# Layer 2's up projections: the passes of the high and the low half of h with the weight's high half made one pass of 512 columns, on one Trainium2 core

## The chip, the cores and the metric

The kernel runs on one core of one Trainium2 chip. The metric is device time in microseconds (us), the median of three runs. Nothing else runs on the chip.

## What is computed

A trunk of two layers over 256 tokens with 2048 features, all in float32. Layer 1 mixes tokens with attention, layer 2 with causal pooling; each layer then has a gated channel mixer, and that of layer 2 is what the change touches:

```python
def conv_ffn(h, w_up, conv_w, conv_b, w_down):     # h 256 x 2048, w_up 2048 x 11264, w_down 5632 x 2048
    u = h @ w_up
    up = jnp.pad(u, ((0, 0), (CONV_WIDTH - 1, 0), (0, 0)))
    y = conv_b
    for i in range(CONV_WIDTH):                    # CONV_WIDTH = 3
        y = y + up[:, i:i + S] * conv_w[i]
    a, g = jnp.split(y, 2, axis=-1)
    return (jax.nn.silu(g) * a) @ w_down
...
mod = cond @ w_mod[l] + b_mod[l]                   # adaLN: shift, scale, gate from c
sh1, sc1, g1, sh2, sc2, g2 = jnp.split(mod, N_MOD, axis=-1)
x = x + g2[:, None, :] * conv_ffn(h, w_up[l], conv_w[l], conv_b[l], w_down[l])
```

## The kernel before

**Split products.** TensorE multiplies in the type fp32r. Each operand is therefore split into a high half (rounded to fp32r) and a low half (the remainder), and a product is made of three passes: high by high, low by high, high by low. The activations are `h_hi` and `h_lo`, the weights `w_hi` and `w_lo`. The helper `sub` holds the three passes of the up projections (L633, L634, L635), each with 256 columns; `unit_tok` holds those of the down projections (L661 to L663), each with 512 columns.

**Units.** Weights arrive in units of 512 rows by 512 columns (1 MB, one DMA of SP into one of the four slots of `raw`). A unit is worked through in two halves. For each half ScalarE writes `w_hi` and VectorE then writes `w_lo` (both in their function `split`), into one of four half-unit slots; the half-unit four places on may be split only when TensorE is done with the old one, which `sub_used` counts. So at the moment when TensorE ends a unit u, the splits stand at the last half of unit u+2, and in the program of ScalarE and VectorE `split(.., j + 2)` stands at the step of unit j.

**Groups, pairs and blocks.** Four units make a group: 512 channels by 256 tokens, in two PSUM banks (`bank_tile`: two tiles of 256 to a bank), slot 0 in banks 0 and 1, slot 1 in banks 2 and 3. A pair (`up_pair`) is a group of a and a group of g, eight units. Layer 2 has three blocks: four pairs and then the down projection of their channels, four pairs and theirs, three pairs and theirs. That makes 11 pairs and 88 up units. The first block is written out pair by pair; the other two run as loops (`Fori`).

**After a group.** ScalarE makes the convolution's last tap with the bias out of PSUM (`conv_last_tap`), VectorE adds the other two taps out of PSUM (`conv_taps`, L1640) and thereby frees the banks (`bank0_free`, `bank1_free`). After a group of g follow the silu (ScalarE), the product with a (VectorE, L1690), `g_hi` (ScalarE) and `g_lo` (VectorE, L1694); only behind them, in the program of both engines, stands the split of the next pair's third unit. Every activation of ScalarE carries the line L1023 of its helper.

**The modulation gate.** In the first block of layer 2 VectorE also works on the last four chunks of `w_mod`, one with each pair: `piece` adds up products (L1376) at the steps 1, 2, 5 and 6 of the pair, L1380 adds the two halves, TensorE sums over the partitions (`gate_sum`, L707, one fp32 matmul that takes its place behind the pair), and VectorE adds the bias (`gate_row`, L1394), behind the `g_lo` of the pair. `gate_sum` writes bank 4, 5 or 6, which the up projections don't use.

The waits that matter here, of TensorE ahead of a group and of `gate_sum`, and VectorE's `gate_row`:

```python
def group_slot_free(g):
    pe.wait_ge(bank0_free, g - 1)
    pe.wait_ge(bank1_free, g - 1)
def gate_sum(c_all, a):
    pe.wait_ge(mod_added, c_all + 1)
    pe.wait_ge(mod_ready, c_all)
...
    dve.wait_ge(mod_red, c_all + 1)
    dve.wait_ge(gate_bias, 16 if c_all < 24 else 32)
    V.tensor_tensor(grow_mlp[...], ps[:, (4, 5, 6, 4)[cg], :],
                    grow_mlp[...], ALU.add).then_inc(mod_ready, 1)
```

Of the kernel before, what the change touches and what calls it, by code (L numbers as in the profile page):

```python
# [22 lines left out]
ALU = mybir.AluOpType  # L23
# [5 lines left out]
P = 128  # L29
# [5 lines left out]
def decoder_trunk(nc, x, c, w_mod, b_mod, norm_gain, w_attn_in, b_forget, w_attn_out, w_pool,  # L35
# [36 lines left out]
    with ExitStack() as ctx:  # L72
# [7 lines left out]
        h_hi = sb("h_hi", [P, KT, SEQ], F32R)  # L80
        h_lo = sb("h_lo", [P, KT, SEQ], F32R)
# [56 lines left out]
        tmpn = work[:, 2048:3072].rearrange("p (t n) -> p t n", t=4)  # L138
        junk = work[:, 2048:3072].rearrange("p (a n) -> p a n", a=QT)
# [35 lines left out]
        def pool_bank(gr, a):  # L175
# [8 lines left out]
                   3: ((2, 3), (4, 5), (6, 7), (2, 3))}  # L184

        GATE_BANKS = {0: (4, 5, 6, 4), 1: (4, 5, 6, 7), 2: (4, 5, 6, 7)}
# [61 lines left out]
        conv_tap = sem("conv_tap")  # L248
        silu_done = sem("silu_done")
# [368 lines left out]
        def _(pe):  # L618
# [46 lines left out]

            def unit_raw(pos):
# [36 lines left out]
            def gate_sum(c_all, a):  # L703

                pe.wait_ge(mod_added, c_all + 1)
                pe.wait_ge(mod_ready, c_all)
                mm(ps[:, (4, 5, 6, 4)[c_all % 4], :], ones[:, :], macc[:, a, 0, :],  # L707
                   start=True, stop=True).then_inc(mod_red, 1)
# [11 lines left out]
            def transposes(n, c):  # L720
# [5 lines left out]
                elif n == 2:  # L726
# [189 lines left out]
            def mlp(l):  # L916
# [4 lines left out]
                def chunk_sum(quad, j):  # L921
                    c = MLP_SUM.get(mlp_step(quad, j)) if l == 0 else None
                    if c is not None and c < 24:
                        gate_sum(c, (c + 1) % 2)
                    elif c is not None:
                        mod_sum(c, (c + 1) % 2, NH)

                for g0, n in BLOCKS:
                    last_block = n == 3

                    def up_pair(i):
                        first = isinstance(i, int) and i == g0 == 0
                        for half in range(2):
                            group_slot_free(g + 2 * i + half)
                            if first and half:
                                pe.wait_ge(t_ready, KT * nm + KT)
                            for ks in range(4):
                                if l == 0:
                                    chunk_sum(q + 2 * i + half, ks)
                                unit(q + 2 * i + half, ks, 4 * ks, ks == 0, ks == 3, h_hi, h_lo, half,  # L940
                                     h_need=KT * nm)
# [12 lines left out]
                    g += 2 * n  # L954
                    if not last_block:
                        for i in range(2):
                            for half in range(2):
                                group_slot_free(g + 2 * i + half)
                                for ks in range(4):
                                    chunk_sum(q + 2 * i + half, ks)  # L960
                                    pe.wait_ge(glo_ready, 2 * (gi + g0 + ks + 1))
                                    unit_tok(q + 2 * i + half, ks, 4 * ks, ks == 0, ks == 3, g_hi, g_lo, half)
                        q += 4
                        g += 4
                    else:
                        for cg in range(4):
                            group_slot_free(g + cg)
                            for ks in range(3):
# [3 lines left out]
                                unit_tok(q + u // 4, u % 4, 4 * ks, ks == 0, ks == 2, g_hi, g_lo, cg % 2)  # L972
# [43 lines left out]
            pe.wait_ge(gate_ready, 8)  # L1016
            gate_rows(2, lambda k: prm[:, FGAIN + k:FGAIN + k + 1])
# [3 lines left out]
        def _(act):  # L1021
# [235 lines left out]
            def conv_last_tap(l, used, dst, first_tile, slot, need):  # L1257
# [3 lines left out]
                for t in range(4):  # L1261
                    A(dst[:, t, :], bank_tile(slot, t), ACT.Identity,
# [3 lines left out]
            def mlp(l):  # L1266
# [8 lines left out]
                for g0, n in BLOCKS:  # L1275

                    def up_pair(i):
                        for half in range(2):
                            for ks in range(4):
# [8 lines left out]
                                if not (first and j < 2):  # L1288
                                    split(q + 2 * i, j + 2)
                                if ks == 3:  # L1290
                                    conv_last_tap(l, 8 * q + 16 * i + 8 * (half + 1), (ya, yg)[half],
                                                  4 * i + (4 * g0 + FT * half), half,
                                                  2 * i + (2 * (gi + g0) + 1))

                        for b in range(2):
                            act.wait_ge((bank0_free, bank1_free)[b], g + 2 * i + 2)
# [46 lines left out]
        def _(dve):  # L1343
# [45 lines left out]
            def gate_row(c_all):  # L1389
# [4 lines left out]
                V.tensor_tensor(grow_mlp[:, 512 * cg:512 * cg + 512], ps[:, (4, 5, 6, 4)[cg], :],  # L1394
# [236 lines left out]

            def conv_taps(l, dst, first_tile, slot, c0):

                for b in range(2):
                    dve.wait_ge(conv_act, c0 + 2 * b + 2)
                    for tap, sh in ((1, 1), (0, 2)):
                        for t in (2 * b, 2 * b + 1):
                            if tap == 0:
                                dve.wait_ge(conv_tap, c0 + t + 1)
                            i = V.scalar_tensor_tensor(  # L1640
                                dst[:, t, sh:SEQ], bank_tile(slot, t)[:, 0:SEQ - sh],
# [4 lines left out]
                    i.then_inc((bank0_free, bank1_free)[b], 1)  # L1646

            def mlp(l):
# [15 lines left out]
                for g0, n in BLOCKS:  # L1664
                    last_block = n == 3

                    def up_pair(i):
                        for half in range(2):
                            for ks in range(4):
# [12 lines left out]
                                if l == 0:  # L1682
                                    chunk_bias(q + 2 * i, j)
                                if ks == 3:
                                    conv_taps(l, (ya, yg)[half], 4 * i + (4 * g0 + FT * half), half,
                                              8 * i + (8 * (gi + g0) + 4 * half))
                        for b in range(2):
                            dve.wait_ge(silu_done, 2 * i + (2 * (gi + g0) + b + 1))
                            dve.wait_ge((bank0_free, bank1_free)[b], g + 2 * i + 1)
# [7 lines left out]
                        if l == 1 and g0 == 0:  # L1697
                            gate_row(i + ch)

# [124 lines left out]
```

## Time and profile before

| | us |
|---|---|
| median of three runs | 2100.67 (2097.5 to 2101.4) |
| the profiled execution | 2103.21 |
| its span, first to last instruction | 2101.6 |
| TensorE busy | 2033.4 (97%) |
| VectorE busy | 1631.1 (78%) |
| ScalarE busy | 1011.7 (48%) |
| mean granted clock of TensorE | 0.992 |

The profile lists each engine's busy time, the groups of instructions by line, and the waits. In a timeline each row gives the start of an instruction (or of several merged ones) in us from the start of the span, its length, the engine, the line and the operation, how many there are, and in brackets the engine's idle time just ahead and what ended it. Matmuls overlap in such rows: the distance between two starts is what one costs, not the length of one.

### The profile page before, as it was taken

What the parts mean: (1) busy time and instruction counts of PE and PEld (TensorE: products, weight loads), DVE (VectorE), ACT (ScalarE), POOL (GpSimd) and SP (SyncE); (2) the same over time, 40 slices, a digit from 0 to 9 for tenths busy, and PEclk for the clock granted to TensorE, in tenths of its full rate; (3) what the DMA queues carried; (4) which work ended last, traced back from release to release, by engine and by line L of the source; (5) the groups of instructions that cost most, each with busy time, mean ns of one, the idle gap of its engine ahead of it and who ended that gap; (6) DMA issues with size and microseconds to landing.
All of it is one profiled execution on the core that took longest, in us unless ns stands there. A gap on an engine that the chain in (4) does not pass through costs nothing.

```text
span 2101.6 us, 36721 instructions
## 1 busy us (share of the span) xinstructions
PE 2033.4 (97%) x13730; PEld 1879.5 (89%) x13730; DVE 1631.1 (78%) x2277; ACT 1011.7 (48%) x1347; POOL 308.0 (15%) x459
## 2 busy tenths in 40 slices
PE   3999999999999999999999999899999999999998
PEld 3888989888999889999899987799988999889986
DVE  5776888887899988898989977888865566555565
ACT  4323674554554444554445555554443454434453
POOL 3232432220111222112212100011000000000000
PEclk9999999999999999999999999999999999999999
DMA  9999899885788999888998874387655555565552
GB/s 360 356 350 330 297 325 322 284 307 203 271 315 315 331 344 340 306 304 314 357 340 309 314 280 149 122 301 280 241 195 186 182 184 185 189 198 164 199 180 100
DMA packets 235842, 558.28 MB, mean 266 GB/s; under 512 B 14024, under 2 KB 15032, under 8 KB 235192
## 3 DMA queue, kind: packets, MB, share of 16 engines
q1 hardware_dynamic: 180408, 355.03, 48.7%
q0 software_dynamic: 55296, 201.35, 26.9%
q8 instruction: 94, 1.54, 0.3%
q14 instruction: 44, 0.36, 0.0%
HBM read 554.23 MB, written 2.10 MB: 265 GB/s over the span
## 4 chain that ended last, share of the span: by engine, by line
PE 83%; DVE 7%; issue 3%; ACT 3%; DMA 3%; SPq 1%; DVEq 0%; ACTq 0%; POOLq 0%
PE ps L633 16%; PE ps L635 15%; PE ps L634 15%; PE ps L661 10%; PE ps L663 10%; PE ps L662 10%; DVE w_lo L1362 2%; PE ps L681 2%; DVE macc L1376 1%; DMA mraw<-in_w_mod 1%; PE ps L699 1%; PE ps L678 1%; ACT w_hi L1023 1%; DMA work<-in_conv_b 1%; DVE work L1640 1%
## 5 line engine op out<-in xcount | busy, mean ns | idle before, releaser
L1023 ACT ACTIVATE w_hi<-raw 128x1024 fp32r<-128x1024 f32 x640 | 666.4, 1056 | 778.9 <-PE ps L635 485.7
L1362 DVE TENSOR_TENSOR w_lo<-raw,w_hi 128x1024 fp32r<-128x1024 f32 x640 | 766.3, 1223 | 346.4 <-ACT w_hi L1023 345.7
L633 PE MATMUL ps<-h_hi,w_hi 128*128 128x256 f32 x3200 | 914.7, 286 | 3.5 <-DVE w_lo L1362 2.9
L635 PE MATMUL ps<-h_hi,w_lo 128*128 128x256 f32 x3200 | 908.1, 284 | 0.0
L634 PE MATMUL ps<-h_lo,w_hi 128*128 128x256 f32 x3200 | 908.1, 284 | 0.0
L633 PEld LDWEIGHTS ps<-h_hi,w_hi 128*128 128x128 f32 x3200 | 616.8, 193 | 7.5 <-issue 6.9
L634 PEld LDWEIGHTS ps<-h_lo,w_hi 128*128 128x128 f32 x3200 | 617.0, 193 | 1.9 <-issue 1.7
L635 PEld LDWEIGHTS ps<-h_hi,w_lo 128*128 128x128 f32 x3200 | 616.7, 193 | 0.0
L1376 DVE SCALAR_TENSOR_TENSOR macc<-mraw,cond,macc 128x512 f32<-128x512 f32 x620 | 427.3, 745 | 50.5 <-DMA mraw<-in_w_mod 43.9
L518 POOL DMA_DIRECT2D mraw<-in_w_mod x358 | 258.7, 723 | 1184.4 <-DVE macc L1376 869.7
L661 PE MATMUL ps<-w_hi,g_hi 128*128 128x512 f32 x832 | 326.1, 392 | 1.5 <-DVE w_lo L1362 1.5
L663 PE MATMUL ps<-w_hi,g_lo 128*128 128x512 f32 x832 | 324.0, 389 | 0.0
L662 PE MATMUL ps<-w_lo,g_hi 128*128 128x512 f32 x832 | 323.8, 389 | 0.0
L661 PEld LDWEIGHTS ps<-w_hi,g_hi 128*128 128x128 f32 x832 | 156.2, 188 | 34.3 <-issue 2.6
L663 PEld LDWEIGHTS ps<-w_hi,g_lo 128*128 128x128 f32 x832 | 156.2, 188 | 32.9
L662 PEld LDWEIGHTS ps<-w_lo,g_hi 128*128 128x128 f32 x832 | 156.3, 188 | 32.0 <-issue 0.2
L1640 DVE SCALAR_TENSOR_TENSOR work<-ps,prm,work 128x255 f32<-128x255 f32 (+1 forms) x352 | 141.0, 472 | 0.0
L1023 ACT ACTIVATE macc<-mraw,cond 128x512 f32<-128x512 f32 x96 | 63.8, 713 | 60.2 <-DMA mraw<-in_w_mod 60.2
L1023 ACT ACTIVATE work<-ps,prm 128x256 f32<-128x256 f32 x176 | 84.3, 558 | 0.0
L1023 ACT ACTIVATE work<-work 128x512 f32<-128x512 f32 (+1 forms) x68 | 40.4, 595 | 68.6 <-DVE work L1640 47.1
L681 PE MATMUL ps<-work,raw 128*128 128x256 f32 x256 | 57.7, 387 | 3.3 <-DMA raw<-in_w_attn_in 3.3
L681 PEld LDWEIGHTS ps<-work,raw 128*128 128x128 f32 x256 | 49.7, 195 | 10.5 <-issue 3.3
(164 smaller groups left out, 1141.3 us busy)
## 6 DMA issues: line engine op xcount, KB each, us to landing
mraw<-in_w_mod POOLq DMA_DIRECT2D x358, 512.0 KB, 6.6
raw<-in_w_up SPq DMA_DIRECT2D x176, 1024.0 KB, 5.7
raw<-in_w_down SPq DMA_DIRECT2D x88, 1024.0 KB, 5.6
raw<-in_w_attn_in SPq DMA_DIRECT2D x48, 1024.0 KB, 9.0
raw<-in_w_attn_out SPq DMA_DIRECT2D x16, 1024.0 KB, 7.0
work<-in_w_mod POOLq DMA_DIRECT2D x12, 512.0 KB, 8.7
early<-in_w_mod POOLq DMA_DIRECT2D x8, 512.0 KB, 12.6
raw<-in_w_pool SPq DMA_DIRECT2D x4, 1024.0 KB, 5.4
```

What stands on the lines that cost most here:

```text
L518: pool.dma_start(slot, w_mod[l, 256 * j:256 * j + 256, ds(512 * c_l, 512)] .rearrange("(k p) n -> p k n", p=P)).then_inc(landed, 16)
L633: mm(o, wh, ah, start=st, stop=False, skip_group_check=True)
L634: mm(o, wh, al, start=False, stop=False, skip_group_check=True)
L635: i = mm(o, wl, ah, start=False, stop=last_half and kk == 1, skip_group_check=True)
L661: mm(o, ah, w_hi[:, s, kk, :], start=st, stop=False)
L662: mm(o, ah, w_lo[:, s, kk, :], start=False, stop=False)
L663: i = mm(o, al, w_hi[:, s, kk, :], start=False, stop=sp_)
L681: i = mm(bank_tile(slot, t), w[:, t * P:(t + 1) * P], xnT[:, k, :], start=st and t % 2 == 0, stop=sp_, skip_group_check=True)
L1023: return nc.scalar.activation(o, i, f, **kw)
L1362: V.tensor_tensor(w_lo[:, s, :, :], raw[:, j % 4, h * 1024:(h + 1) * 1024].rearrange("p (k n) -> p k n", k=2), w_hi[:, s, :, :].bitcast(F3 ...
L1376: V.scalar_tensor_tensor(macc[:, a, kk, :], mod_slot(c_all, j)[:, kk, :], cond[:, k:k + 1], macc[:, a, kk, :], ALU.mult, ALU.add).then_inc ...
L1640: i = V.scalar_tensor_tensor(dst[:, t, sh:SEQ], bank_tile(slot, t)[:, 0:SEQ - sh], prm[:, ds(first_tile + CWcol(l, tap) + t, 1)], dst[:, t ...
```

## The change

In layer 2's up projections the passes L633 and L634 become one. `h_hi` and `h_lo` are now the two halves of one array `h_both`, and one matmul of 512 columns (256 of the high half, 256 of the low) multiplies both with `w_hi`. Its output fills a whole PSUM bank: columns 0 to 255 hold high by high, 256 to 511 low by high. The pass with `w_lo` still has 256 columns and adds into columns 0 to 255. A group so takes four banks instead of two: slot 0 is banks 0 to 3, slot 1 banks 4 to 7.

On the way out ScalarE copies the upper 256 columns into `wide` in SBUF (`wide_copy`, two instructions of 512 elements), VectorE adds the lower ones out of PSUM (`wide_add`, two instructions) and frees the banks, and both the last tap and the other taps read `wide`. `wide` is there once, so the copy waits until the taps of the group before are done (`taps0_done`, `taps1_done`).

As all eight banks are in use, `gate_sum` moves to bank 3: TensorE issues it ahead of the second half of the pair's last unit, VectorE's `gate_row` moves to step 7, between `split` and `wide_add`, and TensorE waits ahead of the next pair, and ahead of the first down projection, until `gate_row` has read the bank. Other banks move along: the transposes at the start of layer 2's channel mixer, the down projections of layer 2 (four slots in turn) and the final gain's rows.

```diff
-        h_hi = sb("h_hi", [P, KT, SEQ], F32R)
-        h_lo = sb("h_lo", [P, KT, SEQ], F32R)
+        h_both = sb("h_both", [P, 2, KT, SEQ], F32R)
+        h_hi, h_lo = h_both[:, 0], h_both[:, 1]
...
-                   3: ((2, 3), (4, 5), (6, 7), (2, 3))}
-        GATE_BANKS = {0: (4, 5, 6, 4), 1: (4, 5, 6, 7), 2: (4, 5, 6, 7)}
+                   3: ((4, 5), (6, 7), (4, 5), (6, 7))}
+        GATE_BANKS = {0: (4, 5, 6, 4), 1: (4, 5, 6, 7), 2: (0, 1, 2, 3)}
...
+            def unit_wide(q, j, k0, first, last, slot, h_need, gate_chunk=None):
+                for h in range(2):
+                    pe.wait_ge(hlo_ready, h_need + k0 + 2 * h + 2)
+                    if h and gate_chunk is not None:
+                        gate_sum(gate_chunk, 0, 3)
+                    low, s0 = split_at(q, j)
+                    pe.wait_ge(lo_ready, low + h + 1)
+                    s = (s0 + h) % 4
+                    for kk in range(2):
+                        k = k0 + 2 * h + kk
+                        for t in range(4):
+                            wh, wl = (w[:, s, kk, t * P:(t + 1) * P] for w in (w_hi, w_lo))
+                            o = ps[:, 4 * slot + t, :]
+                            mm(o.rearrange("p (c n) -> p c n", c=2), wh, h_both[:, :, k, :],
+                               start=first and h == 0 and kk == 0, stop=False, skip_group_check=True)
+                            i = mm(o[:, 0:SEQ], wl, h_hi[:, k, :], start=False, stop=last and h == 1 and kk == 1,
+                                   skip_group_check=True)
+                    i.then_inc(sub_used, 1)
...
+                            if l == 1 and g0 == 0 and not first and half == 0:
+                                pe.wait_ge(mod_ready, i + ch)
...
-                        if l == 1 and g0 == 0:
-                            gate_sum(i + ch, 0)
...
+                    if l == 1 and g0 == 0:
+                        pe.wait_ge(mod_ready, 48)
...
-                                    unit_tok(q + 2 * i + half, ks, 4 * ks, ks == 0, ks == 3, g_hi, g_lo, half)
+                                    unit_tok(q + 2 * i + half, ks, 4 * ks, ks == 0, ks == 3, g_hi, g_lo, half + 2 * l * i)
...
             pe.wait_ge(gate_ready, 8)
+            group_slot_free(G_FFN[1] + 33)
...
+            def wide_copy(used, slot, n):
+                act.wait_ge(sub_used, used)
+                for b in range(2):
+                    if not (isinstance(n, int) and n == 0):
+                        act.wait_ge((taps0_done, taps1_done)[b], n)
+                    A(wide[:, 2 * b:2 * b + 2, :], ps[:, 4 * slot + 2 * b:4 * slot + 2 * b + 2, SEQ:2 * SEQ],
+                      ACT.Copy).then_inc(wide_copied, 1)
...
                 for t in range(4):
-                    A(dst[:, t, :], bank_tile(slot, t), ACT.Identity,
+                    if l and t % 2 == 0:
+                        act.wait_ge((bank0_free, bank1_free)[t // 2], freed)
+                    A(dst[:, t, :], wide[:, t, :] if l else bank_tile(slot, t), ACT.Identity,
...
+            def wide_add(slot, n):
+                for b in range(2):
+                    dve.wait_ge(wide_copied, 2 * n + b + 1)
+                    V.tensor_tensor(wide[:, 2 * b:2 * b + 2, :], ps[:, 4 * slot + 2 * b:4 * slot + 2 * b + 2, 0:SEQ],
+                                    wide[:, 2 * b:2 * b + 2, :], ALU.add).then_inc((bank0_free, bank1_free)[b], 1)
...
                                     split(q + 2 * i, j + 2)
...
+                                if l == 1 and g0 == 0 and j == 7:
+                                    gate_row(i + ch)
+                                if ks == 3 and l == 1:
+                                    wide_add(half, 2 * i + (2 * g0 + half))
                                 if ks == 3:
                                     conv_taps(l, (ya, yg)[half], 4 * i + (4 * g0 + FT * half), half,
...
-                        if l == 1 and g0 == 0:
-                            gate_row(i + ch)
```

## Rows read from the trace of the kernel before

**Rows 1.** Waits of PE, 1450 to 2102 us: in total, times, longest (us).

```profile
PE ps L661 <- DVE w_lo L1362: 0.7, 1, 0.7
```

**Rows 2.** Timeline, PE, an up unit: first passes of two neighbouring units.

```profile
1650.07 0.28 PE L633 MATMUL ps<-h_hi,w_hi 128*128 128x256 f32 x1
...
1655.82 0.28 PE L633 MATMUL ps<-h_hi,w_hi 128*128 128x256 f32 x1
```

**Rows 3.** Timeline, PE, a down projection: two passes, 24 apart.

```profile
1593.63 0.39 PE L661 MATMUL ps<-w_hi,g_hi 128*128 128x512 f32 x1
...
1599.07 0.39 PE L661 MATMUL ps<-w_hi,g_hi 128*128 128x512 f32 x1
```

**Rows 4.** Timeline, PE, first pair of layer 2: starts of its fourth and fifth unit.

```profile
1355.29 0.36 PE L633 MATMUL ps<-h_hi,w_hi 128*128 128x256 f32 x1 [0.71 <-DVE w_lo L1362]
...
1361.53 0.35 PE L633 MATMUL ps<-h_hi,w_hi 128*128 128x256 f32 x1 [0.26 <-DVE w_lo L1362]
```

**Rows 5.** Timeline, DVE: the split that the first wait of rows 4 ended with.

```profile
1353.92 2.36 DVE L1362 TENSOR_TENSOR w_lo<-raw,w_hi 128x1024 fp32r<-128x1024 f32 x2 [0.46 <-ACT w_hi L1023]
```

**Rows 6.** Timeline, PE, end of the first block's second pair.

```profile
1431.44 0.28 PE L635 MATMUL ps<-h_hi,w_lo 128*128 128x256 f32 x1
1431.56 1.02 PE L707 MATMUL ps<-macc,ones 128*128 128x512 f32 x2
```

**Rows 7.** Timeline, ACT, the same end.

```profile
1431.76 1.06 ACT L1023 ACTIVATE w_hi<-raw 128x1024 fp32r<-128x1024 f32 x1 [1.82 <-PE ps L635]
```

**Rows 8.** Timeline, DVE, the same pair: the two halves of macc added.

```profile
1425.24 0.69 DVE L1380 TENSOR_TENSOR macc<-macc 128x512 f32<-128x512 f32 x1
```

**Rows 9.** Timeline, ACT, end of a pair in a loop (second block).

```profile
1705.70 1.06 ACT L1023 ACTIVATE w_hi<-raw 128x1024 fp32r<-128x1024 f32 x1 [1.82 <-PE ps L635]
1706.67 1.91 ACT L1023 ACTIVATE work<-ps,prm 128x256 f32<-128x256 f32 x4
...
1711.27 0.63 ACT L1023 ACTIVATE work<-work 128x512 f32<-128x512 f32 x1 [0.93 <-DVE work L1640]
...
1713.30 2.94 ACT L1023 ACTIVATE w_hi<-raw 128x1024 fp32r<-128x1024 f32 x3
```

**Rows 10.** Timeline, DVE, the same end.

```profile
1706.88 1.23 DVE L1362 TENSOR_TENSOR w_lo<-raw,w_hi 128x1024 fp32r<-128x1024 f32 x1 [1.65 <-ACT w_hi L1023]
1708.03 3.21 DVE L1640 SCALAR_TENSOR_TENSOR work<-ps,prm,work 128x255 f32<-128x255 f32 x8
...
1714.47 3.49 DVE L1362 TENSOR_TENSOR w_lo<-raw,w_hi 128x1024 fp32r<-128x1024 f32 x3 [0.20 <-ACT w_hi L1023]
```

**Rows 11.** Groups of instructions by form, ACT, whole span: count | busy us, mean ns.

```profile
L1023 ACT ACTIVATE work<-ps,prm 128x256 f32<-128x256 f32 x176 | 84.3, 558 | 0.0
...
L1023 ACT ACTIVATE h_hi<-work 128x256 fp32r<-128x256 f32 x64 | 25.5, 418 | 35.3 <-DVE work L1441 34.9
L1023 ACT ACTIVATE work<-ps 128x512 f32<-128x512 f32 x30 | 16.7, 592 | 17.5 <-PE ps L663 6.5 <-PE ps L716 6.4 <-PE ps L825 2.8
...
L1023 ACT ACTIVATE g_hi<-ps 128x256 fp32r<-128x256 f32 x16 | 5.8, 367 | 0.0
```

**Rows 12.** The same view, 1450 to 2102 us, DVE: gate_row.

```profile
L1394 DVE TENSOR_TENSOR work<-ps,work 128x512 f32<-128x512 f32 x2 | 1.4, 684 | 0.0
```

**Rows 13.** Timeline, PE: the only wait of the last two blocks.

```profile
2034.73 0.47 PE L661 MATMUL ps<-w_hi,g_hi 128*128 128x512 f32 x1 [0.70 <-DVE w_lo L1362]
```

**Rows 14.** Timeline, PE: two gaps elsewhere in the kernel.

```profile
79.30 1.02 PE L699 MATMUL ps<-ones,macc 128*128 128x1 f32 x8 [2.23 <-DVE mods L1386]
...
1286.80 2.05 PE L737 MATMUL ps<-ident,work 128*128 128x128 f32 x16 [1.91 <-DVE work L1423]
```

**Rows 15.** Windows behind those gaps: length, PE busy (instructions), PEclk, DMA share, GB/s.

```profile
80.00:84.00 4.00, 4.00 (x26) 0.69 1.04 389
84.00:88.00 4.00, 4.00 (x18) 0.89 1.04 387
...
1288.00:1292.00 4.00, 2.82 (x17) 1.00 0.00 0
```

More of the change, by code:

```diff
@@ L138, in decoder_trunk @@
         tmpn = work[:, 2048:3072].rearrange("p (t n) -> p t n", t=4)
+        wide = work[:, 2048:3072].rearrange("p (t n) -> p t n", t=4)
         junk = work[:, 2048:3072].rearrange("p (a n) -> p a n", a=QT)
@@ L725, in transposes @@
                     pe.wait_ge(gate_ready, 2 * n + 2 * c + 2)
-                elif n == 2:
+                elif n == 2 or n == 3 and c >= 2:
                     pe.wait_ge(t_ready, n * KT + 4 * c - 4)
@@ L923, in chunk_sum @@
                     if c is not None and c < 24:
-                        gate_sum(c, (c + 1) % 2)
+                        gate_sum(c, (c + 1) % 2, (4, 5, 6, 4)[c % 4])
                     elif c is not None:
@@ L939, in up_pair @@
                                     chunk_sum(q + 2 * i + half, ks)
-                                unit(q + 2 * i + half, ks, 4 * ks, ks == 0, ks == 3, h_hi, h_lo, half,
-                                     h_need=KT * nm)
+                                    unit(q + 2 * i + half, ks, 4 * ks, ks == 0, ks == 3, h_hi, h_lo, half,
+                                         h_need=KT * nm)
+                                else:
+                                    unit_wide(q + 2 * i + half, ks, 4 * ks, ks == 0, ks == 3, half, KT * nm,
+                                              i + ch if g0 == 0 and half == 1 and ks == 3 else None)
                                 if first and half == 0 and ks < 2:
                                     transposes(nm, ks + 2)
-                        if l == 1 and g0 == 0:
-                            gate_sum(i + ch, 0)
                     if l == 0 or g0 == 0:
@@ L971, in mlp @@
                                 pe.wait_ge(glo_ready, 2 * (gi + g0 + ks + 1))
-                                unit_tok(q + u // 4, u % 4, 4 * ks, ks == 0, ks == 2, g_hi, g_lo, cg % 2)
+                                unit_tok(q + u // 4, u % 4, 4 * ks, ks == 0, ks == 2, g_hi, g_lo, cg if l else cg % 2)
             mlp(0)
@@ L1292, in up_pair @@
                                                   4 * i + (4 * g0 + FT * half), half,
-                                                  2 * i + (2 * (gi + g0) + 1))
+                                                  2 * i + (2 * (gi + g0) + 1), g + 2 * i + half + 1)
                         for b in range(2):
-                            act.wait_ge((bank0_free, bank1_free)[b], g + 2 * i + 2)
+                            if l == 0:
+                                act.wait_ge((bank0_free, bank1_free)[b], g + 2 * i + 2)
+                            else:
+                                act.wait_ge((taps0_done, taps1_done)[b], 2 * i + (2 * g0 + 2))
                             A(yg[:, 2 * b:2 * b + 2, :], yg[:, 2 * b:2 * b + 2, :], ACT.Silu).then_inc(silu_done, 1)
@@ L1640, in conv_taps @@
                             i = V.scalar_tensor_tensor(
-                                dst[:, t, sh:SEQ], bank_tile(slot, t)[:, 0:SEQ - sh],
+                                dst[:, t, sh:SEQ], (wide[:, t, :] if l else bank_tile(slot, t))[:, 0:SEQ - sh],
                                 prm[:, ds(first_tile + CWcol(l, tap) + t, 1)], dst[:, t, sh:SEQ],
@@ L1734, in mlp @@
                                 cg = u // 3
-                                residual(g + cg, 8 * q + 2 * u + 2, cg % 2, grow_mlp, 512 * cg, gates, before + 2 * cg)
+                                residual(g + cg, 8 * q + 2 * u + 2, cg if l else cg % 2, grow_mlp, 512 * cg, gates, before + 2 * cg)
             def boundary(n, second, third):
```

24 lines of the change are left out of this document (16 added, 8 removed).

## Prediction

> **What bounds the kernel now.** I read the page first: TensorE is busy 97% of the span. An average says little of one stage, so the waits of TensorE came next, from the middle of the changed stage to the end. There is one, of 0.7 us [rows 1]: layer 2's up and down projections run at TensorE's own pace, with VectorE and ScalarE beside them. The third view is the timeline, where the distance between starts shows that pace. A unit of up projections has 48 passes of 256 columns and takes 5.75 us [rows 2], 120 ns a pass. In the down projection 24 passes of 512 columns take 5.44 us [rows 3], 226.7 ns a pass. The granted clock is 1.00 there, which is 2.4 GHz, so the columns take 106.7 and 213.3 ns, and both sizes leave the same 13.3 ns a pass. The last views are the timelines of ScalarE and VectorE where a pair ends: they show how much room the work beside TensorE has. The change takes from TensorE and gives to those two, and adds waits of TensorE on VectorE, so this room decides.
>
> **What the change takes away.** Three passes of 256 columns (360 ns) become one of 512 and one of 256 (226.7 + 120 = 346.7 ns): 13.3 ns saved, 16 times a unit, 0.213 us a unit. For 88 units that is 18.8 us. The first four units of layer 2 gain nothing: their neighbours wait for VectorE already [rows 4], whose pace there is set by the modulation of h and by the pieces of `w_mod`, and a faster pass only lengthens those waits. That leaves 84 x 0.213 = 17.9 us. The trace has no matmul whose moving operand lies in two stretches of 256; I take its fixed part as that of the other 512-column passes, 13.3 ns, the nearest row. The bounds: nothing fixed at all for it (another 18 us saved, which no row supports, since both sizes show the 13.3), or the cost of two passes of 256, 240 ns (nothing saved).
>
> The rows leave 13.3 ns a pass. The Trainium skill, page "TensorE: Matmul & The Clock Gate", section "Back-to-back issue gap", gives columns by 2.4 GHz plus about 2.5 ns for the isolated case. By that figure the estimate of the saving would be 1344 x 2.5 ns = 3.4 us. The rows disagree, at both sizes, and the sum goes by the rows.
>
> **The new wait in the first block, four times.** `gate_row` now stands on VectorE behind both halves of `split(9)`, and the second half can only be split when TensorE has ended the pair's last unit. TensorE must not begin the next pair before `gate_row` is done. Take S as the start of that `w_hi`. TensorE would start its next pass at S - 0.20 [rows 6, 7]. VectorE starts `w_lo` at S + 1.18 and could start the next instruction at S + 2.33 [rows 9, 10]; `gate_row` takes 0.68 us [rows 12] and ends at S + 3.01. From the end of a `w_lo` that TensorE waits for (1353.92 + 1.23 = 1355.15) to the pass are 0.14 us [rows 4, 5], and the first pass costs 0.08 us more than another (0.36 for 0.28). So TensorE loses 3.01 + 0.14 + 0.08 + 0.20 = 3.4 us. Nothing covers it: behind the waiting instruction stand all passes of the next pair, and everything else waits for those. It comes three times between pairs and once ahead of the down projection: 13.7 us. The bounds of one are 3.1 (no 0.14 and no dearer pass) and 3.7 (two more semaphore waits between release and pass, at 0.14 each).
>
> `gate_sum` itself moves from behind the pair to 2.77 us ahead of its end, at the same price. It needs L1380, which ends at 1425.9, 5.6 us ahead of the pair's end [rows 6, 8]. The later taps (next part) push this by some 1.9 us and the faster passes take 0.8 us of the pair; about 1 us is left. Nothing.
>
> **The clock behind those waits.** What a gap of this length does is seen elsewhere. At 77.07 (79.30 - 2.23) TensorE stopped for 2.23 us, then had some 0.9 us of one-column matmuls, 3.1 us without dense work [rows 14]; behind it the granted clock was 0.69 and 0.89 over two stretches of 4 us [rows 15]: 4 x 0.31 + 4 x 0.11 = 1.7 us lost. After 1.91 us and transposes it stayed at 1.00 [rows 14, 15]. The new gaps are 3.3 us with dense passes on both sides, longer than the one that was followed by a lower clock. I take 1.65 us for each of four: 6.6 us. Bounds: 0 and 8.
>
> **The longer chain behind every group.** Before, from S: `w_lo` starts at 1.18, the taps at 2.33, they end at 5.54, the second silu starts at 5.57, ScalarE comes to the `w_hi` of the next pair's third unit at 7.60, and its `w_lo` ends at 1714.47 + 1.23 = S + 10.00 [rows 9, 10]. TensorE wants it at S - 0.20 + 2 x 5.75 = S + 11.3: 1.3 us of room. With the change: ScalarE's copies (592 ns [rows 11]) run beside `w_lo`. VectorE's adds, whose nearest row is `gate_row` with 684 ns [rows 12], start at 2.33 and 2.93 and end at 3.01 and 3.61. ScalarE's last tap starts at 3.10, and VectorE's taps need two of its four tiles. One takes 558 ns from PSUM at a distance of 0.45 [rows 9, 11]; from SBUF I add 0.05, the difference of 418 and 367 for the same 256 elements [rows 11]. So two are done at 3.10 + 0.50 + 0.61 = 4.2, VectorE starts at 4.3 and ends at 7.5, 1.95 us later than before. The path from there on (silu, product, `g_hi`, `w_hi`, `w_lo`) is unchanged, so this `w_lo` ends at S + 11.95. TensorE, now faster, wants it at S - 0.20 + 2 x 5.547 = S + 10.9. With 0.14 and 0.08 on top it loses 1.27 us. In the second and third block that happens behind five pairs: 6.4 us. Behind the second block's last pair the two units are down units of 5.44 us, and the loss is 1.5. Behind the third block's last pair the kernel waits already [rows 13], so the whole 1.95 comes on top. Sum 9.8 us. Bounds, with the lengthening between 1.7 and 2.1: 8 and 11. The four pairs of the first block don't pay, since TensorE is 3.4 us late there. Behind a group of a nothing waits: the same shift meets over 4 us of room there, as no silu and no product stand in between.
>
> **Edits at nothing.** The banks of the transposes, of the down groups and of the final rows: their waits are for work that ended units ago. VectorE and ScalarE get 44 instructions each, some 30 and 26 us beside a TensorE of over 600 us; what of that lies on the path is in the chain above. Transfers need no more than before.
>
> **Sum.** -17.9 + 13.7 + 6.6 + 9.8 = +12.2 us. On the profiled execution (2103.21, its span 2101.6 and 1.6 around it) that gives 2115.4; it ran 2.5 us above the median of the runs, so on the median, 2100.67 + 12.2 = 2112.9 us, 0.6% slower.
>
> **Rivals.** (a) The clock stays up behind the four waits: +5.6 us, 2106.3. For it: 1.91 us left it up, and no row shows a pure gap between 2.3 and 3.2 us. Against it: the row at 79.30. In between lie cases where it falls once to three times; they belong to the forecast's range. (b) The other side: the evictions are hidden. If adds and taps overlap so well that the chain gets longer by less than the 0.7 us at which `w_lo` is still in time (S + 10.7 against S + 10.9), the 9.8 us are gone but for a part of the last pair's, and -17.9 + 13.7 + 6.6 + 0.7 = +3.1 us remain, 2103.8; with the clock up as well, -3.5 us, 2097.2. Against it: the last tap's wait for the add, in series on two engines. (c) The wide pass costs what two cost, because its operand lies in two stretches: nothing saved, +30 us, 2131. For it only that no row shows such an operand. The same mechanism in part is the case in which a pass has a fixed cost of 2.5 ns instead of 13.3, the rest going with the columns: 3.4 saved, 2127. The page "TensorE: Matmul & The Clock Gate" of the Trainium skill, quoted above, has that figure.
>
> **How the numbers follow.** Forecast with one to four falls of the clock, 0.62; clock up, 0.15; evictions hidden, 0.12, half of it with the clock up; wide pass dear, 0.04 (0.02 of it by the figure of 2.5 ns); 0.07 for gains I don't see. The range for 8 in 10: the low end leaves out the hidden evictions with the clock up, and takes the clock-up case with the low bounds, -17.9 + 12.4 + 8 = +2.5, 2103; the high end is all high bounds, -17.9 + 14.8 + 8 + 11 = +15.9, rounded up to 2118 for a saving a little under 13.3 ns. 0.2% is 4.2 us, about what a measurement here can tell from no change. Slower by more: the forecast, two thirds of the clock-up case and the dear pass, 0.76. Within: the rest of clock-up, most of the hidden evictions, 0.14. Faster: 0.10.
>
> **What the profile will show.** Distances of 226.7 and 120 ns in the up units and 5.55 us from unit to unit. Four waits of about 3.2 us of TensorE on L1394's successor (`gate_row`), three ahead of an up pass, one ahead of a down pass, each with a stretch at the lower clock level (1.2 GHz) behind. Seven waits on `w_lo`, about 1.1 us each, ahead of the third unit behind a pair of the second and third block. The second silu starting 7.5 us behind S. What would make it wrong: the order of `gate_row` and `split` on VectorE read wrongly, ScalarE's last tap not held up by the add, or a different distance of the wide passes.

## The result and the profile after

| kernel | median us | ratio to before (95% interval) |
|---|---|---|
| before | 2100.88 | |
| changed | 2116.63 | 1.0082 (1.007 to 1.0094) |

The changed kernel is 15.8 us slower; 2112.9 was forecast. The times here and below leave out one of the seven executions of the kernel with the early split, which had a mean granted clock of 0.455 and took 4474 us. The profiled execution of the changed kernel took 2115.76 us, with a span of 2114.1. The page of that execution, busy time by engine and its share of the span:

```profile
PE 2027.9 (96%) x12322; PEld 1806.0 (85%) x12322; DVE 1659.0 (78%) x2321; ACT 1037.3 (49%) x1391; POOL 308.9 (15%) x459
```

TensorE has 1408 passes less to do and is busy 5.5 us less, yet the span is longer. So the time went into waits, and part of what is still counted as busy into a lower clock. The waits of TensorE from 1300 us on (total, times, longest):

```profile
PE ps L684 <- DVE w_lo L1407: 15.8, 10, 3.2
...
PE ps L665 <- DVE w_lo L1407: 4.1, 2, 2.8
PE ps L665 <- DVE work L1439: 3.0, 1, 3.0
```

Before there was 0.7 us of these in the last 650 us [rows 1], and 1.0 in the first pair [rows 4]. L684 is the wide pass, L665 the first pass of the down projection, L1439 is `gate_row`. A wait is put down to what came last by the records: in three of them it says `w_lo`, although the wait in the program is that on `gate_row`. The timelines of TensorE, ScalarE and VectorE at the end of the first pair show it:

```profile
1379.85 0.28 PE L686 MATMUL ps<-h_both,w_lo 128*128 128x256 f32 x1
1383.29 0.47 PE L684 MATMUL ps<-h_both,w_hi 128*128 128x512 f32 x1 [3.16 <-DVE w_lo L1407]
```

```profile
1380.17 1.06 ACT L1052 ACTIVATE w_hi<-raw 128x1024 fp32r<-128x1024 f32 x1 [2.52 <-PE ps L686]
```

```profile
1381.26 1.22 DVE L1407 TENSOR_TENSOR w_lo<-raw,w_hi 128x1024 fp32r<-128x1024 f32 x1 [2.35 <-ACT w_hi L1052]
1382.40 0.68 DVE L1439 TENSOR_TENSOR work<-ps,work 128x512 f32<-128x512 f32 x1
```

`gate_row` ends at 1383.08, TensorE starts at 1383.29. Without the wait it would have started at 1379.97, 0.12 us behind the start of the last narrow pass. Windows of TensorE over the same place (length, busy and count, granted clock, DMA share, GB/s):

```profile
1380.00:1384.00 4.00, 0.84 (x5) 0.96 0.84 295
1384.00:1388.00 4.00, 4.00 (x16) 0.61 0.73 261
1388.00:1392.00 4.00, 4.00 (x25) 1.00 0.00 0
```

Behind the wait the clock fell to its lower level (1.2 GHz) for part of two stretches: 4 x 0.04 + 4 x 0.39 = 1.7 us. The same came behind the second of these waits and, for longer, around the end of the third, not behind the fourth.

The end of a pair in a loop, with ScalarE first and VectorE below it (they answer to [rows 9, 10]):

```profile
1668.19 1.06 ACT L1052 ACTIVATE w_hi<-raw 128x1024 fp32r<-128x1024 f32 x1 [1.76 <-PE ps L686]
1669.15 1.07 ACT L1052 ACTIVATE work<-ps 128x512 f32<-128x512 f32 x2
1671.38 2.08 ACT L1052 ACTIVATE work<-work,prm 128x256 f32<-128x256 f32 x4 [1.16 <-DVE work L1681]
...
1675.90 0.63 ACT L1052 ACTIVATE work<-work 128x512 f32<-128x512 f32 x1 [0.94 <-DVE work L1692]
...
1677.94 3.90 ACT L1052 ACTIVATE w_hi<-raw 128x1024 fp32r<-128x1024 f32 x4
```

```profile
1669.37 1.23 DVE L1407 TENSOR_TENSOR w_lo<-raw,w_hi 128x1024 fp32r<-128x1024 f32 x1 [1.59 <-ACT w_hi L1052]
1670.51 1.28 DVE L1681 TENSOR_TENSOR work<-ps,work 128x512 f32<-128x512 f32 x2
1672.62 3.25 DVE L1692 SCALAR_TENSOR_TENSOR work<-work,prm 128x255 f32<-128x255 f32 x8 [0.83 <-ACT work L1052]
...
1679.11 4.63 DVE L1407 TENSOR_TENSOR w_lo<-raw,w_hi 128x1024 fp32r<-128x1024 f32 x4 [0.20 <-ACT w_hi L1052]
```

Here S is 1668.19. ScalarE stands idle for 1.16 us until VectorE has added (L1681), VectorE for 0.83 us until ScalarE has made the last tap. The taps start at S + 4.43 (before 2.33), the second silu at S + 7.71 (5.57), and the third unit's `w_lo` ends at S + 12.15 (10.00). TensorE waits:

```profile
1679.19 0.28 PE L686 MATMUL ps<-h_both,w_lo 128*128 128x256 f32 x1
1680.39 0.50 PE L684 MATMUL ps<-h_both,w_hi 128*128 128x512 f32 x1 [0.93 <-DVE w_lo L1407]
```

Last, the pace. A couple of a wide and a narrow pass, read as the distance of wide passes over 32 couples, ahead of the wait at 1680.39 and behind the one at 1726.81:

```profile
1667.64 0.40 PE L684 MATMUL ps<-h_both,w_hi 128*128 128x512 f32 x1
...
1678.95 0.40 PE L684 MATMUL ps<-h_both,w_hi 128*128 128x512 f32 x1
...
1728.65 0.40 PE L684 MATMUL ps<-h_both,w_hi 128*128 128x512 f32 x1
...
1739.74 0.40 PE L684 MATMUL ps<-h_both,w_hi 128*128 128x512 f32 x1
```

The first two rows give 353.4 ns a couple, the other two 346.6. Three passes of 256 columns took 360 ns. The waits cut the stage into eleven stretches of about a pair each. Read in the same way, three of them (the second and third pair, and 1726.81 to 1772.59) ran at 346.7 and the other eight at 353.3. A stretch kept its distance from one wait to the next, but for the eight couples that stand between a `gate_sum` and the end of its pair: they ran at 346.7 in all four pairs of the first block.

### The profile page after: what moved, and what is told of

Its sections match the earlier page's. It is cut to its first block, busy times and chain, and to the rows that moved or that the text cites. A ratio compares the mean times of both kernels' runs of the same rounds, so it can differ in the third digit from the quotient of the medians.

```text
span 2114.1 us, 34059 instructions
## 1 busy us (share of the span) xinstructions
PE 2027.9 (96%) x12322; PEld 1806.0 (85%) x12322; DVE 1659.0 (78%) x2321; ACT 1037.3 (49%) x1391; POOL 308.9 (15%) x459
## 4 chain that ended last, share of the span: by engine, by line
PE 83%; DVE 7%; ACT 4%; issue 4%; DMA 2%; DVEq 0%; POOL 0%; ACTq 0%; POOLq 0%
PE ps L684 13%; PE ps L665 10%; PE ps L667 9%; PE ps L666 9%; PE ps L637 9%; PE ps L638 9%; PE ps L639 9%; PE ps L686 7%; PE ps L705 3%; DVE w_lo L1407 2%; ACT w_hi L1052 2%; PE ps L702 1%; PE ps L723 1%; DVE macc L1421 1%; ACT work L1052 1%
## 5 line engine op out<-in xcount | busy, mean ns | idle before, releaser
L684 PE MATMUL ps<-h_both,w_hi 128*128 128x512 f32 x1408 | 503.6, 402 | 16.5 <-DVE w_lo L1407 15.8
L637 PE MATMUL ps<-h_both,w_hi 128*128 128x256 f32 x1792 | 513.4, 287 | 1.5 <-DVE w_lo L1407 1.3
L638 PE MATMUL ps<-h_both,w_hi 128*128 128x256 f32 x1792 | 508.5, 284 | 0.0
L639 PE MATMUL ps<-h_both,w_lo 128*128 128x256 f32 x1792 | 508.3, 284 | 0.0
L686 PE MATMUL ps<-h_both,w_lo 128*128 128x256 f32 x1408 | 396.8, 282 | 0.0
L637 PEld LDWEIGHTS ps<-h_both,w_hi 128*128 128x128 f32 x1792 | 345.2, 193 | 3.6 <-issue 3.1
L638 PEld LDWEIGHTS ps<-h_both,w_hi 128*128 128x128 f32 x1792 | 345.4, 193 | 1.3 <-issue 1.2
L639 PEld LDWEIGHTS ps<-h_both,w_lo 128*128 128x128 f32 x1792 | 345.4, 193 | 0.0
L684 PEld LDWEIGHTS ps<-h_both,w_hi 128*128 128x128 f32 x1408 | 267.2, 190 | 85.4 <-issue 13.7
L665 PE MATMUL ps<-w_hi,g_hi 128*128 128x512 f32 x832 | 325.9, 392 | 7.7 <-DVE w_lo L1407 4.7
L686 PEld LDWEIGHTS ps<-h_both,w_lo 128*128 128x128 f32 x1408 | 268.4, 191 | 1.0 <-issue 1.0
L665 PEld LDWEIGHTS ps<-w_hi,g_hi 128*128 128x128 f32 x832 | 156.2, 188 | 40.9 <-issue 5.9
L1692 DVE SCALAR_TENSOR_TENSOR work<-work,prm 128x254 f32<-128x254 f32 (+1 forms) x176 | 71.4, 478 | 17.9 <-ACT work L1052 17.9
```

The source lines that it names most:

```text
L637: mm(o, wh, ah, start=st, stop=False, skip_group_check=True)
L638: mm(o, wh, al, start=False, stop=False, skip_group_check=True)
L639: i = mm(o, wl, ah, start=False, stop=last_half and kk == 1, skip_group_check=True)
L665: mm(o, ah, w_hi[:, s, kk, :], start=st, stop=False)
L684: mm(o.rearrange("p (c n) -> p c n", c=2), wh, h_both[:, :, k, :], start=first and h == 0 and kk == 0, stop=False, skip_group_check=True)
L686: i = mm(o[:, 0:SEQ], wl, h_hi[:, k, :], start=False, stop=last and h == 1 and kk == 1, skip_group_check=True)
```

## The experiments

The reasons to be told apart: the four waits on `gate_row` with the clock behind them, the longer chain behind a group, and why most couples take 353.3 ns instead of 346.7. All experiments start from the changed kernel, and those that stand behind the run with both moves from that one. The kernel before, run on the same chip, had 2099.7 us (18 runs), 2099.1 (11) and 2099.7 (15) in the three sessions.

### Do two stretches make the wide pass dearer?

```diff
-        h_both = sb("h_both", [P, 2, KT, SEQ], F32R)
-        h_hi, h_lo = h_both[:, 0], h_both[:, 1]
+        h_both = sb("h_both", [P, KT, 2, SEQ], F32R)
+        h_hi, h_lo = h_both[:, :, 0], h_both[:, :, 1]
...
-                            mm(o.rearrange(...), wh, h_both[:, :, k, :],
+                            mm(o.rearrange(...), wh, h_both[:, k, :, :],
```

> The changed kernel with one difference: h_both is laid out so that the two halves of one k tile lie side by side, and the wide pass reads one stretch of 512. Theory A, two stretches make the wide pass dearer: a wide pass and its narrow one then start 346.7 ns apart in all eleven pairs (now 353.3 in most, 346.7 in some), and about 1000 such couples save 6.7 ns each, 7 us: 2110 us. Theory B, the layout has nothing to do with it (the distance comes from how passes of two lengths alternate): both distances are still there, 2113 to 2119 us. The four waits on gate_row and the seven on w_lo stay the same under both.

2119.0 us, ratio 1.0093 (1.0078 to 1.0108): theory B. Wide passes 32 couples apart, in two stretches of the second block:

```profile
1703.84 0.40 PE L684 MATMUL ps<-h_both,w_hi 128*128 128x512 f32 x1
...
1715.15 0.40 PE L684 MATMUL ps<-h_both,w_hi 128*128 128x512 f32 x1
...
1784.83 0.40 PE L684 MATMUL ps<-h_both,w_hi 128*128 128x512 f32 x1
...
1795.92 0.40 PE L684 MATMUL ps<-h_both,w_hi 128*128 128x512 f32 x1
```

The first two are 353.4 ns apart per couple, the last two 346.6, with the operand in one piece. The layout is not the cause of the long distance. The short distance now stood in other stretches: the third pair, the end of the second block and the end of the third.

### gate_row earlier

```diff
-                                if not (first and j < 2):
+                                if l == 1 and g0 == 0 and j == 7:
+                                    split(q + 2 * i, j + 2, (0,))
+                                    gate_row(i + ch)
+                                    split(q + 2 * i, j + 2, (1,))
+                                elif not (first and j < 2):
                                     split(q + 2 * i, j + 2)
...
-                                if l == 1 and g0 == 0 and j == 7:
-                                    gate_row(i + ch)
```

> The changed kernel with one difference: on VectorE, step 7 of a pair, gate_row stands between the two halves of split(9) instead of behind both. My theory: the four waits of 3.0 to 3.2 us on gate_row vanish (13.5 us), with them the falls of the clock behind them (three, 5 us), and the first block's pairs now show the wait on the third unit's w_lo that the long one covered (about 1.1 us each, 4 us in all): -14.5 us, 2102 us. Rival, the waits are held by something else (the sum of the macc halves, w_lo of the next unit): they only change their releaser, 2114 to 2117 us.

2102.7 us, ratio 1.0019 (1.001 to 1.0028). The waits of TensorE from 1300 us on:

```profile
PE ps L684 <- DVE w_lo L1407: 8.7, 10, 1.0
PE ps L665 <- DVE w_lo L1407: 5.4, 3, 2.9
```

No wait on `gate_row` is left, none of the long ones ahead of L684, and the clock stays at 1.00 through the first block. In their place the first block's pairs wait for the third unit's `w_lo` (0.78, 0.97, 0.95 and 1.18 us), as expected. 13.9 us of the 15.8 (13 by the ratios) hang on where one instruction of 0.68 us stands.

### The next split earlier

```diff
+                        if l == 1:
+                            split(q + 2 * i, 10, (0,))
                         for b in range(2):
...
-                                    split(q + 2 * i, j + 2)
+                                    split(q + 2 * i, j + 2, (1,) if l == 1 and j == 0 else (0, 1))
```

The same on ScalarE and VectorE, and in the down steps.

> The changed kernel with one difference: on ScalarE and VectorE the first half of the split of the unit three places after a pair's end stands ahead of the silu, the product, g_hi and g_lo of that pair, behind the taps. My theory (the longer chain behind a group delays that split): the seven waits on w_lo of 0.9 to 2.8 us in the second and third block vanish, -9 us, 2107.5 us; at most 0.7 us come back in the last block, where g_lo is needed soonest. Rival, VectorE and ScalarE are simply full there, and the order doesn't matter: waits of the same sum with g_lo or a later w_lo as releaser, 2115 to 2118 us.

2107.9 us, ratio 1.0034 (1.0021 to 1.0047). Waits of TensorE from 1300 us on:

```profile
PE ps L684 <- DVE w_lo L1411: 10.9, 5, 3.2
...
PE ps L665 <- DVE work L1443: 3.0, 1, 3.0
PE ps L665 <- DVE g_lo L1759: 0.9, 1, 0.9
```

The seven waits of the second and third block are gone but for 0.9 us on `g_lo`. The engines were not full; the order made the wait.

### The clock: keep TensorE at work while it waits

```diff
+            def filler():
+                for _ in range(4):
+                    mm(ps[:, 0, 0:384], ones[:, :], keep[:, :], start=True, stop=True)
...
+                                filler()
                                 pe.wait_ge(mod_ready, i + ch)
...
+                        group_slot_free(g)
+                        filler()
                         pe.wait_ge(mod_ready, 48)
```

> The changed kernel with one difference: TensorE fills each of the four waits on gate_row with four fp32 matmuls of 384 columns (2.56 us at 2.4 GHz) into bank 0, which nobody reads; the output is the same. Theory: the falls of the granted clock behind the waits come from the idle time, so the clock stays at 1.00 there, the waits shrink to about 0.6 us, the next pass starts at the same time as before: three falls of 1.7 us are saved, -5 us, 2111.5 us. Rival, the clock falls for another reason, or the falls cost nothing on the path: 2115 to 2118 us.

2112.2 us, ratio 1.0064 (1.0051 to 1.0077), 4.5 us below the changed kernel (3.8 by the ratios, whose intervals overlap). The time agrees with the theory but doesn't settle it; the trace does. The end of the first pair on TensorE, and its windows:

```profile
1378.67 2.74 PE L672 MATMUL ps<-keep,ones 128*128 128x384 f32 x8
1381.84 0.50 PE L688 MATMUL ps<-h_both,w_hi 128*128 128x512 f32 x1 [0.43 <-DVE work L1446]
```

```profile
1380.00:1384.00 4.00, 3.57 (x17) 1.00 0.72 225
1384.00:1388.00 4.00, 4.00 (x25) 1.00 0.46 176
```

With work that nobody needs, the clock stays at its upper level (2.4 GHz) behind all four waits. So the falls come from the idle engine. The Trainium skill, page "TensorE: Matmul & The Clock Gate", section "Part 1: The HAM clock gate (the "warmup" mystery)", describes just that: the lower rate is the resting state and activity lifts it. This run agrees. From the first of the four waits to the second TensorE took 49.3 us here and 50.2 in the changed kernel, although 120 of the 128 couples in between ran at 353.3 ns here and at 346.7 there. With that 0.8 us the fall cost 1.7 us, as read from the windows.

Behind another wait the clock did fall in this run. The last wait on `w_lo`, 2.84 us ahead of the third block's down projection, ends at 2040.79:

```profile
2040.00:2044.00 4.00, 3.21 (x10) 0.77 0.22 44
2044.00:2048.00 4.00, 4.00 (x16) 0.81 1.03 395
```

That is 1.7 us again. It happened in the runs with the contiguous layout, with `gate_row` earlier and with the passes in groups too (waits of 2.84, 2.86 and 2.84 us), and not in the changed kernel's profile (2.80 us).

### The passes in groups

```diff
-                        for t in range(4):
-                            ... wide pass of tile t, then narrow pass of tile t
+                        for t in range(4):
+                            ... wide pass of tile t
+                        for t in range(4):
+                            ... narrow pass of tile t
```

> The changed kernel with one difference: for each k tile the four wide passes (one for each tile of 128 output channels) come first and the four narrow ones after them, instead of wide and narrow in turn. Theory C, the 6.7 ns that most couples of a wide and a narrow pass take too long arise where a pass of the one length follows one of the other, and only in some phases of TensorE's start: with a quarter of these changes left, 4 wide and 4 narrow passes take 1387 to 1393 ns instead of 1413, 4 to 5 us less in all: 2112 us. Rival D, each wide pass of this operand is dearer by itself in that phase: the same 1413 ns, 2117 us. The eleven waits stay under both.

2116.3 us, ratio 1.0082 (1.0068 to 1.0095). By the time neither theory is refuted: the runs lie between 2112.0 and 2121.3. In the trace a group of four couples takes 1403 ns from 1655 to 1673 us and from 1925 to 1940 us, which is neither 1387 to 1393 nor 1413. There are two distances again: three of the eleven stretches ran at 1400 ns, the others at 1403. So the order changes the cost, which D alone doesn't say. But C's sum fails as well: a quarter of the changes of length is left, and 13.3 or 16.7 of the 26.7 ns, so the cost doesn't go by the number of changes. Over all couples that is only some 1 us less than in the changed kernel, too little for the times to show.

### Both moves, and both with the groups

> The changed kernel with both moves at once: gate_row between the two halves of split(9), and the first half of the next split ahead of the silu. If the waits on gate_row, the falls of the clock and the waits on w_lo are the whole loss, none of them is left but some 0.9 us for g_lo in the last block, and the kernel keeps what the passes save (6.7 to 13.3 ns for each of 1344): from the 2102.7 us with only the first move, less 7 waits of 1.2 us and 4 of about 1.1 and plus 0.9, 2091 us, ahead of the kernel before (2099.7). Rival: with the order changed the waits show up at other places of the pair, 2098 to 2104 us.

2089.0 us, ratio 0.9948 (0.9935 to 0.9961), ahead of the kernel before by 10 us. All waits of TensorE from 1300 us on in this kernel (L761 is there in every version):

```profile
PE ps L761 <- ACT work L1052: 5.1, 1, 5.1
PE ps L684 <- DVE w_lo L1411: 1.4, 2, 1.0
PE ps L665 <- DVE g_lo L1761: 0.9, 1, 0.9
PE ps L1024 <- DVE work L1490: 0.8, 1, 0.8
```

The waits and the clock behind them were the whole loss. With the passes in groups on top:

> Both moves of the run before and the passes in groups (four wide, four narrow). Theory C: 4 to 8 us below the run with the two moves alone, since the whole 13.3 ns for each couple are saved less a rest: 2085 us. Rival D: the same as that run, 2091 us.

2085.5 us, ratio 0.9939 (0.9926 to 0.9952): the best version, 0.6% under the kernel before. The 3.5 us to the run before it lie within the two intervals, and the groups are worth less than that. Counted from the first transposes of layer 2's channel mixer to the end of the span, which leaves out the part where the two programs are the same, they take 759.3 us and 758.5 us (spans 2089.2 and 2082.5):

```profile
1329.91 3.65 PE L761 MATMUL ps<-ident,work 128*128 128x128 f32 x16 [5.07 <-ACT work L1052]
```

```profile
1324.08 3.48 PE L762 MATMUL ps<-ident,work 128*128 128x128 f32 x16 [5.07 <-ACT work L1053]
```

In the kernel with both moves alone, some 390 of the 1344 couples behind the first four units have 346.7 ns and the others 353.3; in groups all have 350.8, which makes 0.8 us.

### The wide pass undone, the rest kept

```diff
-                            mm(o.rearrange(...), wh, h_both[:, :, k, :], start=..., stop=False, ...)
+                            mm(o[:, 0:SEQ], wh, h_hi[:, k, :], start=..., stop=False, ...)
+                            mm(o[:, SEQ:2 * SEQ], wh, h_lo[:, k, :], start=False, stop=False, ...)
```

> The kernel with both moves (gate_row and split early), and the wide pass undone alone: two passes of 256 columns take its place, each with its own half of h and its own half of the bank, the rest (banks, copies, adds, order) stays. Nothing waits in that kernel but the first pair, so the difference to the run with the two moves is what the wide pass itself is worth. By the distances of its trace (346.7 ns a couple in the first block, 353.3 in the others, 360 for three passes) that is 0.7 x 1344 x 6.7 + 0.3 x 1344 x 13.3 = 11.6 us: 2100.5 us, about the kernel before. By my forecast's 13.3 ns throughout it would be 17.9 us: 2107 us. Rival: the third instruction costs nothing here since something else sets the pace, 2089 to 2093 us.

2100.1 us, ratio 1.0001 (0.9992 to 1.001). The wide pass is worth 2100.1 - 2089.0 = 11.1 us, and not 17.9. The two medians come from different sessions, but the stage alone says the same: here it takes 2095.5 - 1324.7 = 770.8 us, 11.5 more than with the wide pass (759.3); the kernel before takes 770.4. So the copies, the adds and the other banks cost 0.4 us at most once the order is mended.

```profile
1324.71 3.44 PE L763 MATMUL ps<-ident,work 128*128 128x128 f32 x16 [5.08 <-ACT work L1054]
```

### All passes of one length

```diff
-                            i = mm(o[:, 0:SEQ], wl, h_hi[:, k, :], ...)
+                            i = mm(o.rearrange(...), wl, h_both[:, :, k, :], ...)
```

> The kernel with both moves, and the narrow pass made a wide one too (w_lo with both halves of h, which adds the product of the two low halves that the kernel otherwise leaves out). All passes of the up projections then have 512 columns and no length changes. Theory C (the 6.7 ns come where the length of the pass changes): two passes take 453.3 ns in all pairs, as in the down projection. Theory D (a wide pass with this operand is dearer by itself): 460 ns or more in the second and third block. The time is the run with the two moves and 1344 x 0.1 to 0.113 us more: 2232 (C) to 2242 us (D).

2228.7 us (two executions), ratio 1.0617 (1.0598 to 1.0636). Two wide passes of L684, with 15 others of it and 16 of L686 between them:

```profile
1699.64 0.39 PE L684 MATMUL ps<-h_both,w_hi 128*128 128x512 f32 x1
...
1706.89 0.39 PE L684 MATMUL ps<-h_both,w_hi 128*128 128x512 f32 x1
```

32 passes in 7.25 us are 226.6 ns each, and so it is at every place read in all three blocks. The same wide pass, with the same operand in two stretches, has its 13.3 ns as soon as its neighbours are as long as it is. Theory D is out, and the narrow pass isn't dear by itself either: among passes of its own length it takes 120 ns, in the run before this one. The extra cost needs both lengths, as theory C says, though not by C's sum, as the groups showed.

## Why the prediction was right and where it was wrong

The direction, the place and the mechanism of each wait came out as forecast; the step that failed is a term of the sum, the saving. For the size I compare the stage alone, from the first transposes of layer 2's channel mixer on (before, then after), since the two profiled executions differ by 5 us ahead of it, where they run the same instructions:

```profile
1331.23 3.37 PE L737 MATMUL ps<-ident,work 128*128 128x128 f32 x16 [5.07 <-ACT work L1023]
```

```profile
1326.17 3.34 PE L761 MATMUL ps<-ident,work 128*128 128x128 f32 x16 [5.08 <-ACT work L1052]
```

To the end of the span that is 770.4 us before and 787.9 after, +17.6 us, against the forecast's +12.2.

| term | forecast us | read from the trace us |
|---|---|---|
| saved by the wide pass | -17.9 | -11.5 |
| four waits on gate_row | +13.7 | +13.5 |
| falls of the clock | +6.6 | +5.7 |
| waits on the third unit's w_lo | +9.8 | +9.7 |
| sum | +12.2 | +17.4 |

**The saving is the step that failed.** The prediction gave the wide pass the fixed part of the other 512-column passes, "the nearest row". Those rows have neighbours of the same length. Three pairs at 13.3 ns for each of 128 couples are 5.1 us, eight pairs at 6.7 ns, less the first four units, are 6.4. The bounds of this term held the value, but the range of the sum allowed only for "a little under 13.3 ns", and the couples saved 8.6 on average. That the median still lay under the top of the range, 2118, is in part luck: the stage alone lost 17.6 us, more than the +15.9 of all high bounds, and the medians are 15.8 apart. I named only an operand in two stretches, and a fixed part of 2.5 ns, as what could make the saving smaller; the contiguous layout and the run with all passes wide exclude the first, and a saving of 11 us instead of 3.4 excludes the second. What was missing is the mix of lengths. The run with three passes confirms its size: 11.1 us, 11.5 by the stage.

**The four waits** were 3.16 us three times and 3.01 once; with the 0.16 us between where the next pass would have started and where the wait begins in the records, as in 1383.29 - 1379.97 = 3.32, and a dearer first pass they cost 13.5. Their price followed from the order on VectorE alone.

**The clock** fell behind three waits of four, and behind two, two and three in the runs with the contiguous layout, the groups and the early split, 10 of 16 in all. "Four times" was one too many. The prediction put nothing down for the clock behind the longest of the `w_lo` waits, of 2.8 us; it cost nothing in the changed kernel's profile, but the clock fell there in four of the five runs that have it. The price of one is 1.6 us by the time from the first of these waits to the second (50.22 us, less 44.37 for 128 couples of 346.7 ns, 0.87 for `gate_sum` and 3.41 for the wait), and some 2.5 behind the third, where it was low for longer. What decides whether it falls after a gap of 3.2 us isn't settled by these runs.

**The chain** was forecast to make the third unit's `w_lo` end at S + 11.95; it ended at 12.15. TensorE's pace was slower than assumed, which gave 0.2 us back, and it started 0.05 us behind that `w_lo` instead of 0.14, so a wait cost 1680.39 - 1679.31 = 1.08 us and a first pass dearer by 0.09, 1.17 instead of 1.27. The last one came to 2.80 where before had 0.70 [rows 13]. The rival that adds and taps overlap is out: both engines stood idle for each other in turn.

**Edits at nothing** cost nothing: no wait of TensorE on a bank shows, and `gate_sum` in the last unit ran without one.

## What to carry to other kernels

When an engine that sets the pace gets a new wait, ask where the releasing instruction stands in its own queue: an instruction of 0.7 us that stood behind a split which needs TensorE's last pass cost 3.4 us each time, plus the clock, and moving it up by one place brought back 13 to 14 us. A gain on the bounding engine that is paid with longer chains on the others is kept only if the order there is mended in the same change: this one lost 15.8 us alone and won 10 with two moves in the order. And take the price of an instruction from rows with the same neighbours, not from a row of the same size.

## What the runs showed of the hardware that I had not expected

A pass in fp32r has 13.3 ns beyond its columns as long as all passes around it have the same length: 120.0 ns at 256 columns, 226.7 at 512, both in the kernel before. Where a pass of 512 and one of 256 take turns, the couple has 346.7 or 353.3 ns. In groups of four and four, four couples took 1400 or 1403 ns.

The distance changed only where TensorE had waited or where other passes stood in between, and which pairs have which differs from kernel to kernel. Behind a wait both occurred. Behind `gate_sum`, an fp32 matmul, it was the short one all 24 times in the six kernels where wide and narrow take turns (the changed one, the contiguous layout, both moves apart and together, the filler); behind a down projection it was the long one all 12 times. In the kernel with both moves TensorE waits for nothing between its first pair and its last down projection. Its first `gate_sum` stands at 1380.06; here are wide passes 24 couples apart, ahead of it and behind it:

```profile
1367.34 0.40 PE L684 MATMUL ps<-h_both,w_hi 128*128 128x512 f32 x1
...
1375.82 0.40 PE L684 MATMUL ps<-h_both,w_hi 128*128 128x512 f32 x1
...
1381.27 0.40 PE L684 MATMUL ps<-h_both,w_hi 128*128 128x512 f32 x1
...
1389.59 0.40 PE L684 MATMUL ps<-h_both,w_hi 128*128 128x512 f32 x1
```

They give 353.3 and 346.7 ns. From there the first block kept 346.7 to its end, and the other two ran at 353.3 throughout. What inside TensorE makes the two distances stays open, and with it whether an order could be found that holds the short one.
